# Six linear layers of a second block in three products of split operands, on one Trainium2 core

## What is computed

```python
h = rms_norm(x, norm1_g)
xm, o_pre, gate_pre, xl, lru_gate, merge_pre = split(h @ w_in)
y_m = sigmoid(o_pre) * rms_norm(mlstm(conv(xm), gate_pre + b_gates), norm_g)
y_l = (lru_forward(conv(xl)) + lru_backward(conv(xl))) * gelu(lru_gate)
g_m, g_l = split(sigmoid(merge_pre))
merged = g_m * (y_m @ w_branch_mlstm) + g_l * (y_l @ w_branch_lru)
x = x + merged @ w_out
x = x + peer(rms_norm(x, norm2_g))     # product keys, gathered expert rows
return rms_norm(x, final_norm_g)
```

## Time and profile before

| | us |
|---|---|
| median of 3 runs | 2819.59 |
| lowest and highest | 2817.48, 2819.62 |
| the profiled execution | 2812.28 |
| its span, first to last instruction | 2810.5 |
| routing, up to the first expert product | 706 to 742 |
| experts | 742 to 1754 |
| second block up to the end of `w_out` | 1754 to 2115 |
| `peer` and the last norm | 2115 to 2810 |

### The profile page before, as it was taken

One profiled execution on the slowest core, in us unless ns is written; L12 is line 12 of the kernel. 1 busy time (PEld: TensorE's weight loads), 2 busy tenths in 40 slices (PEclk: granted clock), 3 DMA queues, 4 the chain that ended last, 5 costly groups with the idle time before them and its releaser, 6 DMA issues.

```text
span 2810.5 us, 33021 instructions
## 1 busy us (share of the span) xinstructions
PE 2597.5 (92%) x12361; PEld 2035.2 (72%) x12361; DVE 2007.5 (71%) x2922; ACT 1188.3 (42%) x1220; POOL 252.7 (9%) x281
## 2 busy tenths in 40 slices
PE   9989999999899999999999999988998997887877
PEld 7888998798788888888888888877886543332332
DVE  5775543875798888888898887436605887788875
ACT  1444332253577777767677775122501110111010
POOL 0000000000000000000000000000001433333331
PEclk9999999999899999999999999999999999999999
DMA  6543554540699999999999996632446999999997
GB/s 207 164 135 106 183 183 125 163 135 31 235 363 338 351 351 349 356 330 370 333 357 345 352 352 240 201 102 84 150 150 239 405 421 421 421 421 422 421 421 315
DMA packets 335917, 776.22 MB, mean 276 GB/s; under 512 B 21952, under 2 KB 154176, under 8 KB 302784
## 3 DMA queue, kind: packets, MB, share of 16 engines
q1 hardware_dynamic: 298080, 503.94, 51.6%
q0 software_dynamic: 36864, 268.45, 23.0%
q10 hardware_dynamic: 864, 2.38, 0.2%
HBM read 773.67 MB, written 1.05 MB: 276 GB/s over the span
## 4 chain that ended last, share of the span: by engine, by line
PE 74%; DMA 12%; DVE 10%; issue 2%; ACT 2%; DVEq 0%; POOL 0%; ACTq 0%
DMA dense_weights<-in_peer_rows,work 12%; PE banks L751 12%; PE banks L753 12%; PE banks L752 12%; PE banks L570 8%; PE banks L629 5%; PE banks L1121 4%; PE banks L592 4%; PE banks L593 4%; PE banks L596 4%; DVE dense_weights L2420 1%; PE banks L1084 1%; PE banks L514 1%; PE banks L898 1%; PE banks L814 1%
## 5 line engine op out<-in xcount | busy, mean ns | idle before, releaser
L2074 DVE TENSOR_TENSOR weight_tiles_low<-weight_tiles,weight_tiles_high 128x2048 fp32r<-128x2048 f32 x334 | 758.7, 2289 | 129.2 <-ACT weight_tiles_high L1552 128.1
L1552 ACT ACTIVATE weight_tiles_high<-weight_tiles 128x2048 fp32r<-128x2048 f32 x332 | 634.6, 1917 | 172.9 <-DMA weight_tiles<-in_moe_w_down 94.0
L1121 PE MATMUL banks<-dense_weights,work 128*128 128x512 f32 x952 | 460.0, 636 | 117.4 <-DVE work L2430 117.3
L1121 PEld LDWEIGHTS banks<-dense_weights,work 128*128 128x128 f32 x952 | 187.4, 202 | 378.5 <-issue 211.9
L751 PE MATMUL banks<-weight_tiles_high,gathered_parts 128*128 128x512 f32 x896 | 354.9, 396 | 3.7 <-issue 3.7
L753 PE MATMUL banks<-weight_tiles_high,gathered_parts 128*128 128x512 f32 x896 | 350.1, 391 | 0.0
L752 PE MATMUL banks<-weight_tiles_low,gathered_parts 128*128 128x512 f32 x896 | 349.4, 390 | 0.0
L2420 DVE CUSTOM_DVE_ANT_0 dense_weights<-dense_weights,banks 128x1024 f32<-128x1024 f32 x238 | 286.0, 1218 | 83.4 <-DMA dense_weights<-in_peer_rows,work 81.5
L1336 POOL DMA_INDIRECT dense_weights<-in_peer_rows,work x238 | 224.3, 943 | 736.9 <-DVE work L2389 369.8
L1799 DVE TENSOR_TENSOR weight_tiles_low<-weight_tiles,weight_tiles_high 128x2048 fp32r<-128x2048 f32 x73 | 167.0, 2291 | 137.4 <-ACT weight_tiles_high L1357 136.4
L1742 ACT ACTIVATE work<-work 128x2 f32<-128x2 f32 x129 | 26.2, 203 | 559.5 <-DVE work L2420 559.1
(11 more groups left out here) (392 smaller groups left out, 3809.7 us busy)
## 6 DMA issues: line engine op xcount, KB each, us to landing
weight_tiles<-in_moe_w_gate SPq DMA_DIRECT2D x112, 1024.0 KB, 5.2
weight_tiles<-in_moe_w_up SPq DMA_DIRECT2D x112, 1024.0 KB, 5.2
weight_tiles<-in_moe_w_down SPq DMA_DIRECT2D x112, 1024.0 KB, 4.8
weight_tiles<-in_w_in SPq DMA_DIRECT2D x38, 1024.0 KB, 5.6
weight_tiles<-in_w_xkv SPq DMA_DIRECT2D x16, 1024.0 KB, 5.5
weight_tiles<-in_ffn_w_gate SPq DMA_DIRECT2D x11, 1024.0 KB, 5.4
weight_tiles<-in_ffn_w_up SPq DMA_DIRECT2D x11, 1024.0 KB, 5.4
weight_tiles<-in_ffn_w_down SPq DMA_DIRECT2D x11, 1024.0 KB, 4.8
```

The lines of the kernel that those rows point to most:

```text
L1121: mm = pe.matmul(halves[half], diag[(first + j) % 8], pair_row(first + j)[:, 1, half * 512:(half + 1) * 512], start=False, stop=end and j ...
L1552: act.activation(high_tile(j), raw_tile(j), ACT.Copy).then_inc(g.high, 1)
L2074: dve.tensor_tensor(low_tile(j), raw_tile(j), high_tile(j).bitcast(F32), ALU.subtract).then_inc(g.split, 1)
```

## The change

Six layers of the second block, `o_pre`, `gate_l`, `branch_m`, `merge_l`, `branch_l` and `w_out`, are computed in the split form: 24 groups. `xm`, `xl` and `merge_m` stay plain. Their inputs are split too. The normed input (`xn_high`, `xn_low`), y_m (`hM_high`, `hM_low`), y_l (`hl_high`, `hl_low`) and `merged` are rounded on ScalarE and get their low part on VectorE, with semaphores on which TensorE waits slice by slice (`arrived`). Calls of `round_ahead` and `low_ahead` are put at chosen places of ScalarE's and VectorE's programs; where a `ready` would round tiles too early, it is a bare wait now. The output gating of y_l is done in four pieces. Buffers: the high parts of activations lie behind the three slots of the high ring, the spatial weights and biases of the first block are one tensor whose place is used again, and `std4` lies in `work`. In the routing the four put copies stand ahead of the low parts of tiles 2 and 3.

```diff
             def split_linear(key, who, x, dmas=1):
+                for g in split_groups(key, who, x, dmas):
+                    pass
+
+            def split_groups(key, who, x, dmas=1):
                 for g in range(4):
                     tile = split_tile(KT, 2 * P, dmas)
                     bank = G.begin(who, (key, g))
                     G.end(split_group(bank, tile, (P, P), *x))
                     G.free()
+                    yield g
+
+            def arrived(tiles, sem_, per):
+                def x(k):
+                    pe.wait_ge(sem_, k // per + 1)
+                    return tiles[:, k, :]
+                return x
...
-                o_pre = linear_groups("o_pre", "a", 4, x)
+                o_pre = split_groups("o_pre", "a", (arrived(xn_high, xn_rounded, 1), arrived(xn_low, xn_split, 1)))
...
-                linear("gate_l", "a", 4, x)
+                split_linear("gate_l", "a", x)
                 lru_gates(1, ("r", "i"), range(4))
                 G.freed[gates_at - 2] = G.freed[gates_at - 1] = (group_done, G.total)
-                pe.wait_ge(ym_ready, 1)
-                linear("branch_m", "v", 4, lambda k: hM[:, k, :])
+                split_linear("branch_m", "v", (arrived(hM_high, ym_rounded, KT), arrived(hM_low, ym_split, KT)))
...
-                linear("merge_l", "a", 4, x)
-                pe.wait_ge(yl_ready, 1)
-                linear("branch_l", "v", 4, lambda k: h_l[:, k, :])
-                pe.wait_ge(merged_ready, 4)
-                linear("w_out", "v", 4, lambda k: merged[:, k, :])
+                split_linear("merge_l", "a", ((lambda k: xn_high[:, k, :]), (lambda k: xn_low[:, k, :])))
+                split_linear("branch_l", "v", (arrived(hl_high, yl_rounded, 2), arrived(hl_low, yl_split, 2)))
+                split_linear("w_out", "v", (arrived(merged_high, merged_rounded, 2), arrived(merged_low, merged_split, 2)))
...
+                for k in range(KT):
+                    act.wait_ge(x_ready, KT * (N_NORMS - 1) + k + 1)
+                    act.activation(xn_high[:, k, :], xF[:, k, :], ACT.Copy).then_inc(xn_rounded, 1)
                 for g in range(4):
                     ready(("xm", g))
                     take(act.activation(xm_pad[:, 2 * g:2 * g + 2, 2:2 + SEQ], pair(banks_of(("xm", g))), ACT.Copy))
+                round_ahead(("o_pre", 0))
...
+                        act.wait_ge(ym_ready, 1)
+                        act.activation(hM_high, hM, ACT.Copy).then_inc(ym_rounded, 1)
+                        round_ahead(("gate_l", 0))
+                    else:
+                        round_ahead(("branch_m", 0))
...
+                    round_ahead((("gate_l", "branch_m")[d], 1))
                     act.wait_ge(lru_v_ready, d + 1)
                     act.activation(lru_t[:, :, :], lru_t[:, :, :], ACT.Sqrt).then_inc(lru_s_ready, 1)
...
-                    for j in (2, 3):
-                        low_part(0, j)
                 for e in range(4):
                     dve.wait_ge(g.group_done, g.after["put", e])
                     took_it(dve.tensor_copy(put[:, e, :], bank_in(("put", e))[:, 0:SEQ]))
+                if n == 0:
+                    for j in (2, 3):
+                        low_part(0, j)
...
                 dve.tensor_tensor(g_sum, g_b, g_max, ALU.add).then_inc(a_ready, 1)
+                low_ahead(("o_pre", 1))
...
                 dve.tensor_tensor(hM, hM, o_sig, ALU.mult).then_inc(ym_ready, 1)
+                low_ahead(("r", 0, 0))
...
+                    if d == 0:
+                        dve.wait_ge(ym_rounded, 1)
+                        dve.tensor_tensor(hM_low, hM, hM_high.bitcast(F32), ALU.subtract).then_inc(ym_split, 1)
+                    low_ahead((("gate_l", "branch_m")[d], 0))
...
-                dve.tensor_tensor(h_l, h_l, gate_l, ALU.mult).then_inc(yl_ready, 1)
+                for g in range(4):
+                    s = slice(2 * g, 2 * g + 2)
+                    dve.tensor_tensor(h_l[:, s, :], h_l[:, s, :], gate_l[:, s, :], ALU.mult).then_inc(yl_ready, 1)
+                low_ahead(("branch_m", 3))
```

More of the change, by code:

```diff
@@ L1662, in lru_gate @@
                 for g in groups:
-                    ready((name, d, g))
+                    act.wait_ge(group_done, G.after[name, d, g])
                     for i in range(2):
@@ L1689, in lru @@
                     if d == 0:
-                        copies("gate_l", gate_l, func=ACT.Gelu)
+                        for g in range(4):
+                            round_ahead(("gate_l", min(g, 2)))
+                            act.wait_ge(group_done, G.after["gate_l", g])
+                            take(act.activation(gate_l[:, 2 * g:2 * g + 2, :], pair(banks_of(("gate_l", g))), ACT.Gelu))
             def merge():
+                round_ahead(("branch_m", 3))
                 act.wait_ge(gated_ready, 2)
                 copies("merge_l", g_l, func=ACT.Sigmoid)
+                act.wait_ge(group_done, G.after["branch_m", 3])
+                for g in range(4):
+                    s = slice(2 * g, 2 * g + 2)
+                    act.wait_ge(yl_ready, g + 1)
+                    act.activation(hl_high[:, s, :], h_l[:, s, :], ACT.Copy).then_inc(yl_rounded, 1)
+                for g in range(4):
+                    s = slice(2 * g, 2 * g + 2)
+                    round_ahead(("branch_l", g))
+                    act.wait_ge(merged_ready, g + 1)
+                    act.activation(merged_high[:, s, :], merged[:, s, :], ACT.Copy).then_inc(merged_rounded, 1)
             def peer():
@@ L2308, in lru @@
                     ins.then_inc(lru_v_ready, 1)
+                    low_ahead((("gate_l", "branch_m")[d], 1))
                     edge = 0 if d == 0 else SEQ - 1
@@ L2329, in merge @@
             def merge():
-                dve.wait_ge(yl_ready, 1)
+                low_ahead(("merge_l", 3))
+                for g in range(4):
+                    s = slice(2 * g, 2 * g + 2)
+                    dve.wait_ge(yl_rounded, g + 1)
+                    dve.tensor_tensor(hl_low[:, s, :], h_l[:, s, :], hl_high[:, s, :].bitcast(F32), ALU.subtract).then_inc(yl_split, 1)
                 dve.wait_ge(act_took, G.took["merge_l", 3])
@@ L2333, in merge @@
                 for g in range(4):
+                    low_ahead(("branch_l", g))
                     ready(("branch_l", g))
@@ L2340, in merge @@
                     dve.tensor_tensor(merged[:, s, :], merged[:, s, :], pair_tmp, ALU.add).then_inc(merged_ready, 1)
+                for g in range(4):
+                    s = slice(2 * g, 2 * g + 2)
+                    dve.wait_ge(merged_rounded, g + 1)
+                    dve.tensor_tensor(merged_low[:, s, :], merged[:, s, :], merged_high[:, s, :].bitcast(F32), ALU.subtract).then_inc(merged_split, 1)
                 add_to_residual("w_out")
```

38 lines of the change are left out of this document (29 added, 9 removed).

## The result

The changed kernel takes 2842.95 us (median of 4 runs, 2841.25 to 2844.79), the kernel before beside it 2818.8 us (4 runs). The ratio is 1.0083 with an interval of 1.0070 to 1.0095: 24 us slower, where +6.9 us was forecast, and outside the range of 2817 to 2834. The profiled execution took 2841.25 us against 2812.28, so 29.0 us have to be found.

A forecast was written before the change was run, and what follows sets the result against it. TensorE was taken to bound the touched stretch almost alone, with new low parts making it wait. Terms -2.85 + 1.1 + 8.6 = +6.9 us on the profiled 2812.28, with the median 7.3 above, gave 2826.5 us, range 2817 to 2834.

The forecast's parts named there:

- (d): Second block: 1.2 GHz through the first group after both waits, gate columns delayed by low parts; 2836 us, chance 0.07.
- Routing: Ahead of the first expert: put copies first let TensorE start at 739.4; -2.85 us, bounds -1 and -3.7.
- `o_pre`: Second block: a low part ahead of the convolution delays convolution, Silu and `qM`; +1.1 us, bounds -1.2 and +3.
- First direction: LRU: TensorE waits 10.5 us for `gate_l`'s first low part, ready at 1978.6; restart costs 1.9, bounds 1.2 and 2.5.
- Second direction: LRU: Tanh waits for `branch_m` tiles until 2021.1; TensorE waits some 6 us for `merge_l`'s low part, ready at 2050.4.
- End of `w_out`: End of the second block's split layers: 2123.5 against 2114.95, +8.6 us.
- The pace of a split group: TensorE in the 24 groups: 5.76 us instead of 6.91, saving 1.15 each, 27.6 in all.
- Rival (a): Split layers: ScalarE and VectorE keep ahead, TensorE stays the bound; -30.5 us, 2789, chance 0.09.

The follow-up runs named there:

- b_pad24: Kernel before with only 24 words (96 bytes) of padding behind the ring of high parts; 2842.6 us, ratio 1.0091.
- b_put: Kernel before with only the routing's put copies moved ahead of the low parts of tiles 2 and 3; 2812.47 us, ratio 1.0000.
- a_aligned: Changed kernel with 128 words of padding instead of 24 and the small tensors behind `work`; 2820.89 us, ratio 1.0016.
- a_gate_l_first: a_aligned with `gate_l` low parts 0, 1 ahead of the head norm's reciprocal, 2, 3 ahead of y_m's; 2809.6 us, ratio 0.9982.
- a_both_orders: a_gate_l_first with Tanh and Exp ahead of `branch_m` roundings, `merge_l` low parts 0, 1 right behind scan and sum; 2803.18 us, ratio 0.9956.
- b_work_aligned: Kernel before with the small tensors behind the work area, so `work` starts at a multiple of 512 bytes; 2815.6 us, ratio 1.0002.
- b_pad128: Kernel before with 128 words (512 bytes) of padding behind the ring of high parts; 2813.73 us, ratio 0.9990.

## Why the prediction was wrong, point by point

- **The failing step** is a term left out of the sum: "-2.85 + 1.1 + 8.6 = +6.9". It has no term for the experts, where the profile has over a third of the whole span. The text on the change told that buffers were laid out anew, and the prediction put their price at nothing without a reason or bounds. It measures +23.9 us in the changed kernel, and b_pad24 shows nearly all of it by itself: 2.90 an expert in the trace, 23 us, and 17 to 34 us by its interval. With a layout that keeps the experts' pace the change gives 2822.41 beside 2817.32: +5.1 us by the medians, 4 to 12 by the interval, which has +6.9 in it. No rival had the mechanism either; (d), 2836, was too low still and had another cause.
- **Routing**, -2.85: right in its size. -2.3 in the changed kernel and -3.0 in b_put, and TensorE is now let go by ScalarE's put copies, as forecast (TensorE's timeline; before):

```profile
738.81 0.79 PE L781 MATMUL banks<-weight_tiles_high,gathered_parts 128*128 128x512 f32 x1 [0.75 <-ACT squares L1573]
```

- **`o_pre`**, +1.1: inside its bounds. -0.6 in the changed kernel, +0.9 in a_aligned (69.57 against 68.69). Single executions scatter, but five of the eight traces with the old form have 68.7 and four of the six with the new one 69.6 to 69.8, so +1.0 is the likely size. That the 4.6 us saved on TensorE are worth nothing there held.
- **First direction**: a wait of 10.5 forecast, 10.01 measured. The whole second block is 19.3 us later, by the square of `hM` (1955.89 before, 1975.16 after). Less that shift, the first low part is ready at 1979.5 (forecast 1978.6). The restart was a little dearer than the 1.9 taken. The row at 0.50 shows half clock, the first group takes 2006.85 - 1998.83 = 8.02 us, and the next ones start 5.76 apart: 2.3 us lost, inside the bounds of 1.2 to 2.5.
- **Second direction**: Tanh forecast at 2021.1, measured at 2041.22 - 19.3 = 2021.9, behind two waits for weight tiles. The low part of `merge_l` is ready at 2070.1 - 19.3 = 2050.8 (2050.4), the wait is 6.25 (some 6). Two more waits inside `branch_m`, 3.93 and 2.54, weren't named one by one, but its end is at 2063.92 - 19.3 = 2044.6 (near 2044).
- **End of `w_out`**: 2143.75 - 19.3 = 2124.5 against 2123.5. The stage costs +9.5, forecast +8.6; 0.4 of the gap is the first restart, and the second one, ahead of `merge_l`, adds about as much. Against the 160.4 of most other traces it costs +8.2, so the agreement is good to a little over 1 us and no better.
- **The pace of a split group**, 5.76 us, held in the new groups between the waits (5.73 in `w_out`). By the Trainium skill (TensorE: Matmul & The Clock Gate, Back-to-back issue gap) an estimate of 5.24 us had stood beside it. That section gives the formula for an isolated matmul and says that in a stream with weight loads it is too low at small N and too high at large N. Each product here has a weight load, and at 256 columns the trace lies above the estimate, as 2010.69 - 2004.93 = 5.76 shows.
- **Rival (a)** was refused because of two waits. a_gate_l_first and a_both_orders show that the reading was right and also how far it goes: the waits are matters of order, and without them the split form gains. It gains 10 to 11 us in that stage, about half of the 20 x 1.15 = 23 us that its groups save. Waits for low parts of 4.9 us remain; the other 7 to 8 us were not divided up.

## What to carry to other kernels

A change that moves the start of a tensor can change the pace of every matmul that reads it, also in stages that the diff doesn't touch: list which tensors move and by how much, and compare the period of the longest untouched loop first. Here a stationary operand at a multiple of 512 bytes kept the full pace, and one that was 96 or 128 bytes off did not; a smaller multiple, such as 256 bytes, was not tried. A sum of the edits should have a row for the stages with most of the span, with a bound, even where nothing in them was edited. Where a split form trades matmul time for work on two other engines, it paid here only once that work filled their idle time *ahead* of the product that wants it; put it in front of a wait, not behind what the wait is for.

## What the runs showed of the hardware

The speed of 128x512 products in fp32r depends on where the stationary 128x128 operand begins in its partition. With 336 such products and five groups of transposes in the gate and up half: 78.83 us at the old place, 78.84 with 512 bytes added, 80.44 with 128, 81.06 with 96, so up to 2.8%. The down half goes from 47.04 us at a multiple of 512 bytes over 47.34 at the old place to 48.02. Plain fp32 products do not show it: the sixteen records of the scatter, whose stationary operand lies in `work`, take 3.72 us before and after, in the rows of the two experts above. Why the place matters stays open. The mean time of a product's record rises by 5 to 8 ns, but weight loads have records of 188 to 189 ns in all of these kernels, so their rows don't show it, and no run took the path of the load by itself. Whether fp32r products of 128x256 are as sensitive to the place of their stationary operand wasn't tried.

The moving operand gives no such clear picture. In the feed-forward it is the weight slices that are stationary, and they weren't moved. In its gate and up groups the high part of the activations lies in the ring of high parts and wasn't moved either; the low part, a third of the products, lies in `gathered_parts` and was, and the groups start 5.76 us apart before and 5.75 after. In its down products, 528 of 128x256, both parts of the moving operand lie in `work_parts`. From the first of them to the next stage, the kernel before and b_work_aligned:

```profile
396.17 0.36 PE L751 MATMUL banks<-work_parts,weight_tiles_high 128*128 128x256 f32 x1 [1.09 <-DVE dense_weights L1978]
...
458.44 3.61 PE L514 MATMUL banks<-squares,ones 128*128 128x256 f32 x16
```

```profile
396.01 0.36 PE L751 MATMUL banks<-work_parts,weight_tiles_high 128*128 128x256 f32 x1 [1.09 <-DVE dense_weights L1978]
...
459.43 3.62 PE L514 MATMUL banks<-squares,ones 128*128 128x256 f32 x16
```

That is 62.27 us before and 63.42 with `work` at a multiple of 512 bytes, where the experts are fastest; b_pad128 takes 59.94 and the changed kernel 61.69. So this stretch changes with the layout too, by up to 3.5 us and not in the same direction. The place of `work` alone doesn't set it: b_pad24 and the changed kernel have the same place and take 62.27 and 61.69. What does was not tested.
